# Two key tiles' sample logits, and two tiles' sample value products, in one step instead of one tile at a time

## The reference, cut to what matters

```
idx    = top_k(indexer_scores(qi, wi, ki_all), 256)
k_sel, v_sel = gather(cache_k, idx), gather(cache_v, idx)
logits = einsum('bthd,btkhd->bhtk', q, k_sel) * scale + bias
p      = softmax(masked logits)
out    = einsum('bhtk,btkhd->bthd', p, v_sel)
```

## Time and profile before

| what | value |
|---|---|
| median of 3 runs | 1876.94 us (1875.51 to 1877.05) |
| span of the profiled execution | 1871.8 us |
| the attention stage in it | about 515 to 968 us |
| PE busy over the span | 92% |

### The profile page before, as it was taken

One profiled execution on the slowest core, in us unless ns is written; L12 is line 12 of the kernel. 1 busy time (PEld: TensorE's weight loads), 2 busy tenths in 40 slices (PEclk: granted clock), 3 DMA queues, 4 the chain that ended last, 5 costly groups with the idle time before them and its releaser, 6 DMA issues.

```text
span 1871.8 us, 28982 instructions
## 1 busy us (share of the span) xinstructions
PE 1726.3 (92%) x11176; PEld 1413.1 (75%) x11176; DVE 859.4 (46%) x1839; ACT 653.4 (35%) x1374; POOL 603.9 (32%) x715
## 2 busy tenths in 40 slices
PE   7888999989967778898789999999999999999998
PEld 6553464789944455565555689999999999999997
DVE  4571889757734444566531343323132323232324
ACT  4464786577232233343321121222222222222123
POOL 1100334266354665555513140404040404040400
PEclk9799999989987899998889999999999999999999
DMA  8301202111184655655571001111110101020202
GB/s 242 93 1 49 92 31 78 49 35 42 43 270 149 177 173 160 175 152 152 149 260 66 0 1 46 46 46 45 39 50 29 60 20 70 10 80 3 98 1 96
DMA packets 68965, 158.03 MB, mean 84 GB/s; under 512 B 9402, under 2 KB 25518, under 8 KB 68608
## 3 DMA queue, kind: packets, MB, share of 16 engines
q1 hardware_dynamic: 47488, 84.91, 13.7%
q0 software_dynamic: 21376, 71.75, 12.8%
HBM read 144.14 MB, written 12.49 MB: 84 GB/s over the span
## 4 chain that ended last, share of the span: by engine, by line
PE 82%; DVE 6%; issue 4%; another core or an unknown queue 3%; ACT 3%; POOL 2%; DMA 1%; SPq 0%; DVEq 0%; ACTq 0%; POOLq 0%
PE psum L1819 7%; PE psum L1817 7%; PE psum L1806 7%; PE psum L1807 7%; PE psum L1805 7%; PE psum L1818 7%; PE psum L1746 6%; PE psum L1360 5%; PE psum L1524 4%; PE psum L1373 3%; PE psum L1549 2%; PE psum L1663 2%; PE psum L1340 2%; PE psum L1641 2%
## 5 line engine op out<-in xcount | busy, mean ns | idle before, releaser
L1805 PE MATMUL psum<-n_hi,wup_hi 128*128 128x384 f32 (+1 forms) x768 | 251.3, 327 | 0.0
L1817 PE MATMUL psum<-h_hi,wdn_hi 128*128 128x384 f32 (+1 forms) x768 | 250.9, 327 | 0.0
L1807 PE MATMUL psum<-n_hi,wup_lo 128*128 128x384 f32 (+1 forms) x768 | 250.8, 327 | 0.0
L1806 PE MATMUL psum<-n_lo,wup_hi 128*128 128x384 f32 (+1 forms) x768 | 250.8, 327 | 0.0
L1819 PE MATMUL psum<-h_hi,wdn_lo 128*128 128x384 f32 (+1 forms) x768 | 250.2, 326 | 0.0
L1818 PE MATMUL psum<-h_lo,wdn_hi 128*128 128x384 f32 (+1 forms) x768 | 250.1, 326 | 0.0
L2441 DVE TENSOR_TENSOR h_lo<-h_full,h_hi 128x384 fp32r<-128x384 f32 (+1 forms) x96 | 112.5, 1184 | 261.5 <-ACT h_hi L1221 252.8
L1213 ACT ACTIVATE hrelu<-psum 128x384 f32<-128x384 f32 (+1 forms) x96 | 45.5, 474 | 502.0 <-PE psum L1807 502.0
L2446 DVE TENSOR_TENSOR x_region<-psum,x_region 128x384 f32<-128x384 f32 (+1 forms) x192 | 102.8, 536 | 252.9 <-PE psum L1819 251.8
L905 POOL TENSOR_TENSOR wup_lo<-wup_full,wup_hi 128x4096 fp32r<-128x4096 f32 x8 | 72.3, 9037 | 421.0 <-ACT wup_hi L1197 421.0
L1075 ACT ACTIVATE arena<-x_region,arena 128x384 bf16<-128x384 f32 (+2 forms) x192 | 166.5, 871 | 23.3 <-POOL arena L851 23.3
(11 more groups left out here) (329 smaller groups left out, 3155.1 us busy)
## 6 DMA issues: line engine op xcount, KB each, us to landing
wup_full<-in_w_up SPq DMA_DIRECT2D x8, 2048.0 KB, 8.0
wdn_full<-in_w_down SPq DMA_DIRECT2D x8, 2048.0 KB, 7.7
arena<-in_x_prompt SPq DMA_DIRECT2D x16, 512.0 KB, 8.8
arena<-in_w_in SPq DMA_DIRECT2D x3, 2048.0 KB, 8.4
arena<-in_w_in SPq DMA_DIRECT2D x12, 512.0 KB, 5.6
out<-arena SPq DMA_DIRECT2D x17, 256.0 KB, 4.5
arena<-in_w_out SPq DMA_DIRECT2D x8, 512.0 KB, 8.4
out<-arena SPq DMA_DIRECT2D x8, 512.0 KB, 2.7
```

The source lines that it names most:

```text
L1805: pe.matmul(b, wu_hi[:, k, col], n_hi[:, k, o:o + w], start=(k == 0), stop=False)
L1806: pe.matmul(b, wu_hi[:, k, col], n_lo[:, k, o:o + w], start=False, stop=False)
L1807: i = pe.matmul(b, wu_lo[:, k, col], n_hi[:, k, o:o + w], start=False, stop=(k == KT - 1))
L1817: pe.matmul(b, wd_hi[:, f, col], h_hi[:, hf, 0:w], start=(f == 0), stop=False)
```

## The change

`k_logits` no longer runs for each tile in its own odd unit. In every second odd unit (x % 4 == 3) it runs for the even tile and then the odd one. The value products of tiles 2j and 2j + 1 both run in the unit that had tile 2j alone; the last sequence keeps one tile a unit. Since the first tile's logits are later, the near page's slot of the K ring is now given back by the first transpose of tile 1 and not by the first matmul of tile 0's logits.

```diff
-VAL_AT = {SEQU * b + VLAG + 2 * x: (b, x) for b in range(LAST) for x in range(NPAGE_TILES)}
+VAL_AT = {SEQU * b + VLAG + 4 * j: [(b, 2 * j), (b, 2 * j + 1)] for b in range(LAST) for j in range(4)}
...
-del TURN_AT[END + 2], VAL_AT[END + 3], VAL_AT[END + 5], LAST_VALUE[END + 6]
+del TURN_AT[END + 2], VAL_AT[END + 3], LAST_VALUE[END + 6]
 TURN_AT[END + 1] = LAST - 1, 3
-VAL_AT[END + 2], VAL_AT[END + 3] = (LAST - 1, 6), (LAST - 1, 7)
+VAL_AT[END + 2] = [(LAST - 1, 6), (LAST - 1, 7)]
...
-VAL_AT.update({END + 6 + x: (LAST, x) for x in range(NPAGE_TILES)})
+VAL_AT.update({END + 6 + x: [(LAST, x)] for x in range(NPAGE_TILES)})
...
                         i = pe.transpose(bank(4 + kk)[:, k * P:(k + 1) * P], kring[:, s, kk, k * P:(k + 1) * P], ident)
+                        if t == 1 and kk == 0 and k == 0:
+                            i.then_inc(k_used, 1)
...
-                i = pe.matmul(bank(6)[:, c:c + P], slotrow[:, t, :], MKT[:, b, :], start=True, stop=False, skip_group_check=True)
-                if t == 0:
-                    i.then_inc(k_used, 1)
+                pe.matmul(bank(6)[:, c:c + P], slotrow[:, t, :], MKT[:, b, :], start=True, stop=False, skip_group_check=True)
...
-                if b < DB and x % 2:
+                if b < DB and x % 4 == 3:
+                    k_logits(b, x // 2 - 1)
                     k_logits(b, x // 2)
...
-                if u in VAL_AT:
-                    vals(*VAL_AT[u])
+                for tile in VAL_AT.get(u, []):
+                    vals(*tile)
```

## The result

The changed kernel takes 1937.01 us (median of 4 runs, 1928.81 to 1942.87) against 1876.22 us (4 runs, 1874.89 to 1877.05) for the kernel before beside it: ratio 1.0329, 95% interval 1.0303 to 1.0355. It is slower by 61 us. The forecast was 1876.5 us, no change, in a range up to 1889; the time lies far outside it.

A forecast was written before the change was run, and what follows sets the result against it. The prediction looked to PE, busy 360 of the attention stage's 453 us, as the bound. Its terms, -5.5 + 1.6 + 2.5 + 1.0 + 0 = -0.4 us, took 1876.94 to 1876.5 us; range 1866 to 1889.

The forecast's parts named there:

- The V side: V ring: slots return earlier, rows needed 6 to 7 us earlier; POOL is ahead, PE gains nothing; taken 0.
- rival 5: POOL's gathers: V slots return in pairs, runs of eight become twelve, PE held up; +17 us, 1894; chance 0.13.
- The sum of the local terms: Attention stage: gain at odd tiles' waits against losses of cover, -5.5 + 1.6 + 2.5 + 1.0 + 0 = -0.4 us.
- the range's lower end, 1866: Whole kernel: fast end of the forecast range, said to lie between two faster rivals; about 0.05 chance beyond it.
- both rivals, 1870 and 1867: Attention stage: 1870, gain without the loss, chance 0.19; 1867, hold-ups halved at three of seven sequences, chance 0.10.
- Gain at the odd tile's wait: L1549 waiting for DVE's copy: even tile's logits fill the gap; 5.5 us gained, waits 22.6 to about 17.
- Loss of cover: Between e=0's and e=1's turns: moved block no longer hides other engines' work; 5.1 us lost, bounds 2.5 to 17.3.
- Work: PE's logits and value products: none removed or added; L1549 and L1622 stay at 46.6 and 53.4 within 2 us.
- The sign for rival 5: ACT's waits for L1524: the longest, 8.38 us before, would grow or vanish; vanishing would instead suggest hold-ups moving.
- Clock: PE's granted clock, 0.88 before: would follow idle time down if e=1's turn waits in most late pairs; chance 0.15.

The follow-up runs named there:

- after_sp_v: Changed kernel with its 120 V ring loads moved off POOL to plain loads of consecutive rows in SP's queue; 1797.18 us, 0.9592 of the kernel before.
- sp_v: Kernel before with 120 V ring loads moved off POOL to plain loads of consecutive rows in SP's queue; 1784.23 us, ratio 0.9571.
- plain_kv: Kernel before with all 256 of POOL's K and V ring loads as plain loads of consecutive rows, still on POOL; 1763.84 us, ratio 0.9468.
- bunched: Kernel before with even tiles' V gathers held until two units later, giving runs of eight, PE's program untouched; 1951.53 us, ratio 1.0448.
- after_paced: Changed kernel with each V gather of the first seven sequences also waiting for the next tile's k_turn; 1889.11 us, 1.0133 of the kernel before.
- half_width: Kernel before with each V gather fetching half the bytes a row, 256 of 512 floats, as many gathers; 1861.12 us, ratio 0.9979.
- plain_v: Kernel before with V's ring loads as plain loads of consecutive rows, still issued by POOL, K still gathered; 1767.88 us, ratio 0.9437.

## Why the prediction was wrong

**The step that failed** is "The V side ... Taken: 0". Its reason, that POOL is ahead and PE gains nothing from earlier slots, looked for rows that come too late. None did. What mattered was how many gathers POOL issues in one run, and that PE is held up in it. The same step's doubt was written down as rival 5, *longer runs of gathers*: the mechanism was right (slots in pairs, runs of eight that become ten and twelve; three tiles' gathers free at once), the size was not. It was priced at half of 5 us in each of seven sequences, +17; measured are 61. Two terms were missing. The price was taken for the added gathers alone, but runs of four became runs of eight and ten too (31 of four fell to 10). And POOL, held up by a PE that is late, came late for K too: its waits for L1524 rose from 37.9 to 94.2 us, more than those for V did. The argument against the rival, that other unbroken runs pass with PE at work, was wrong in kind: runs of four do (PE busy for 87% of them), long ones from their fifth gather on do not (53%).

In PE's own account the loss has two halves, and the sum had a term for neither: PE is idle for 37 us more in the stage (130 against 93), of which the tails of long runs hold 34 (57.5 against 23.9), and its busy time is 32 us longer, 12.5 of them in L1549. How much of the longer busy time is the lower clock, 0.82 against 0.88, and how much is matmuls going out one by one, the rows don't split.

**The sum of the local terms** (-0.4 us) has two measurements near it: `logits_only`, which moves only the logits, has +4.5 us, and `after_sp_v`, at 1.0022 of `sp_v`, about +4 us, with overlapping intervals. It was too kind by 4 to 5 us at most, inside its own bounds. Two slips in it don't matter: the 5.1 us between span and median are not all time outside the program (1942.87 beside a span of 1941.1, and 1.7 to 2.0 us in every execution for which both are on record), but they cancel in the difference; and the range's lower end, 1866, lies below both rivals, 1870 and 1867, and not between them. By its parts, in the changed kernel, where the hold-ups lie over all of them:

- Gain at the odd tile's wait: L1549's waits for the copy were to fall from 22.6 to about 17; they are 14.0 in 7 waits. The direction is right; the size isn't confirmed, since the same line now has 20.5 us of "issue" before it.
- Loss of cover: L1663's waits for DVE's copy (L2314, now L2315) were to grow from 3.9 to 8 or 9; they are 8.0, as forecast. That L1663 would wait 24.5 us for ACT's L1136 was not foreseen: in five waits of up to 7.8 us, one of them at 773.00, just past a run of ten gathers (757.38 to 769.96):

```profile
773.00 0.45 PE L1663 MATMUL psum<-arena 128*128 128x128 f32 x1 [7.78 <-ACT arena L1136]
```

- Work: L1622 kept its 53.4 us (53.3). L1549 went from 46.6 to 59.1, beyond the 2 us allowed: its matmuls go out one by one. `logits_only` has 57.7 there at almost no cost, so this figure was a poor sign.
- The sign for rival 5 was that ACT's longest wait for L1524 grows: 8.3 to 12.5 us. It did.
- Clock: the granted clock of the stage fell from 0.88 to 0.82, with more idle time on PE. It is 0.99 in `plain_kv`, where PE is busy for 91% of the stage, and 0.81 in `bunched`. But it doesn't rank the kernels: `after_paced` has 0.91 and is slower than the kernel before.

**What stays open.** What in PE a gather holds up is not shown. It isn't the bytes moved (`half_width`), nor a load issued by POOL as such (`plain_v`), nor a semaphore that PE's rows name. The rows show matmuls that go out one by one with gaps of "issue", and results that come later than PE's rows have them. The Trainium skill, "SBUF — State Buffer", section "SBUF: two separate sides", says that a transfer can't slow an engine's operation and that PE's access to SBUF waits for no one. By that rule, pacing the gathers would be worth nothing; measured are 0.990 to 1.045 with PE's program unchanged. The runs don't show that it is SBUF where PE is held, so they don't refute the rule on ports, but it must not be read as "gathers are free for PE". Nor is it settled what `after_paced` lacks. It isn't the number of its long runs: the kernel before has 10 as well, and PE's idle time from their fifth gather on is no longer (21.7 us against 23.9). That PE's delay begins with the fifth gather, and not with the time since the run began, no run separates.

## What to carry to other kernels

When an edit changes when ring slots come free, ask how many gathers the issuing engine can then run off without a break, and look in the timeline at what the other engines complete meanwhile; here slots given back one by one, or one `wait_ge` that spaces the gathers (0.990), decided more than the order of the matmuls. A wait that spaces them is no gain in itself: a second one gave all of it back (0.9996). A wait that the profile can't name ("remote", "issue") and that ends when another engine's run of work ends is a cause to be tested and priced, not a curiosity. And where an index list is known to be consecutive, plain loads can take the gathers' place: 0.944 here, though for other rows than this kernel needs.

## What the runs showed of the hardware

- While GpSimd issues a long run of indirect loads (128 rows each, 0.95 us and a gap of 0.30), TensorE's instructions go out one by one (six matmuls in 3.8 us, where sixteen take 0.65) and their results reach ScalarE up to 8.3 us after the end that TensorE's rows give (701.66 against 709.97).
- It goes with the place in the run: TensorE is busy for 84 to 89% of the time in the first four gathers of long runs, and for 47 to 53% from the fifth on (kernels before, after and `bunched`). 27 runs of eight or more in place of 10 cost 4.5%; 3 in place of 10, with 50 runs of four in place of 31, gain 1.0%. With 1 in place of 10 and more standing of GpSimd nothing is gained (0.9996).
- Signals between other engines are on time in such runs: VectorE starts 0.03 us after ScalarE's row (663.16, 663.19).
- What V's loads are worth by form: half the bytes in each gather 0.2%; 120 of them as plain loads of consecutive rows in SP's queue 4.3%; all 128 as such loads, still from GpSimd, 5.6%, at 592 ns of GpSimd for one.
